# Giving V rows of zero weight an out-of-bound index in a gather-heavy encoder step

## The reference

```
s = jnp.einsum('thcd,hcnd->thcn', q, sub_keys).astype(jnp.float32)
...
top_s, pos = lax.top_k(cand, PEER_TOPK)
expert = jnp.take_along_axis(cidx, pos, axis=-1)
g = jax.nn.softmax(top_s, axis=-1)
u = u_table[expert]
hid = jax.nn.gelu(jnp.einsum('thkd,td->thk', u, xblk).astype(jnp.float32), approximate=False)
v = v_table[expert]
return jnp.einsum('thk,thkd->td', (g * hid).astype(xblk.dtype), v)
```

## Time and profile before

| | |
|---|---|
| median of 3 runs | 3290.63 us (3286.97 to 3292.52) |
| profiled execution, first to last instruction | 3284.0 us |
| POOL busy | 2107.1 us (64%) |
| DVE busy | 1965.5 us (60%) |
| PE busy | 1896.7 us (58%) |
| moved by DMA | 1285.39 MB, 391 GB/s over the span |
| of it by the gathers' queue (q0) | 1143.35 MB in 314032 packets, 88.2% of the DMA engines' time |

### The profile page before, as it was taken

How to read it: one execution, slowest core, us unless ns; L and a number is a source line. 1 busy time by engine, 2 the same in 40 slices (tenths; PEclk the granted TensorE clock), 3 DMA queues, 4 the chain that set the end, 5 groups by cost and what they waited for, 6 DMA issues and landing times. The chain is left out here.

```text
span 3284.0 us, 24041 instructions
## 1 busy us (share of the span) xinstructions
PE 1896.7 (58%) x7901; PEld 735.9 (22%) x7901; DVE 1965.5 (60%) x4492; ACT 348.4 (11%) x787; POOL 2107.1 (64%) x2190
## 2 busy tenths in 40 slices
PE   8976856746843386577543486577644333333546
PEld 4454412333310033332200022322200000000001
DVE  1599695596678844865486744864587645453120
ACT  2221201121100111210100101210100000000000
POOL 0156477566567765775577765775677777777775
PEclk9986978867966588788766698678766665656779
DMA  7699999999999999999999999999999999999998
GB/s 259 228 388 340 404 382 386 402 409 396 405 407 408 386 406 404 409 407 406 398 396 408 396 406 404 410 407 406 388 403 409 387 410 409 409 409 410 409 410 340
DMA packets 384892, 1285.39 MB, mean 391 GB/s; under 512 B 38904, under 2 KB 44672, under 8 KB 384768
## 3 DMA queue, kind: packets, MB, share of 16 engines
q0 software_dynamic: 314032, 1143.35, 88.2%
q1 hardware_dynamic: 68272, 131.60, 11.0%
q10 hardware_dynamic: 2464, 8.91, 0.7%
HBM read 1273.98 MB, written 9.44 MB: 391 GB/s over the span
## 5 line engine op out<-in xcount | busy, mean ns | idle before, releaser
L1069 DVE CUSTOM_DVE_ANT_0 ring<-ring,ps 128x1024 f32<-128x1024 f32 x1088 | 1304.1, 1218 | 990.6 <-DMA ring<-in_peer_u_dram,u_idx 964.7
L1436 PE MATMUL ps<-ring,spread 128*32 128x512 f32 x4352 | 847.1, 892 | 1172.2 <-DMA ring<-in_peer_v_dram,v_idx 1163.1
L706 POOL DMA_INDIRECT ring<-in_peer_u_dram,u_idx x1088 | 1040.0, 956 | 598.3 <-issue 273.7
L706 POOL DMA_INDIRECT ring<-in_peer_v_dram,v_idx x1088 | 1060.5, 975 | 476.6 <-issue 287.0
L1489 PE MATMUL ps<-wbuf,actT 128*128 128x512 f32 (+2 forms) x1536 | 671.8, 592 | 8.0 <-ACT actT L823 3.9
L1436 PEld LDWEIGHTS ps<-ring,spread 128*32 128x32 f32 x4352 | 157.4, 141 | 1779.2 <-DMA ring<-in_peer_v_dram,v_idx 1135.5
L1489 PEld LDWEIGHTS ps<-wbuf,actT 128*128 128x128 f32 (+1 forms) x1536 | 281.8, 189 | 404.8 <-issue 394.3
L1128 DVE MAX8 work<-work 128x8 f32<-128x128 f32 (+3 forms) x432 | 109.2, 322 | 48.5 <-ACT work L994 46.3
L1132 DVE FIND_INDEX8 work<-work 128x8 uint32<-128x128 f32 (+3 forms) x432 | 133.3, 328 | 0.0
L776 ACT COPY spread<-weightT 128x16 f32<-128x16 f32 x64 | 14.2, 224 | 912.7 <-PE ps L1436 872.6
L1069 DVE DVE_READ_ACCUMULATOR2_ANT hidden<- 128x1 f32 x1088 | 89.7, 82 | 0.0
(11 more groups left out here) (189 smaller groups left out, 1179.9 us busy)
## 6 DMA issues: line engine op xcount, KB each, us to landing
wbuf<-in_w_in_dram SPq DMA_DIRECT2D x55, 1024.0 KB, 11.7
wbuf<-in_peer_w_q_dram SPq DMA_DIRECT2D x40, 1024.0 KB, 11.7
wbuf<-in_w_out_dram SPq DMA_DIRECT2D x20, 1024.0 KB, 11.7
ring<-in_peer_u_dram,u_idx POOLq DMA_INDIRECT x1088, 11.6
ring<-in_peer_v_dram,v_idx POOLq DMA_INDIRECT x1088
x_v<-x_scratch ACTq DMA_DIRECT2D x8, 512.0 KB, 6.9
out_dram<-x_v ACTq DMA_DIRECT2D x8, 512.0 KB, 7.3
x_in<-in_x_prompt_dram SPq DMA_DIRECT2D x7, 512.0 KB, 19.6
```

The costliest lines, as they stand in the source:

```text
L706: pool.indirect_dma_start(ring[:, at % RING, :], None, table, bass.IndirectOffsetOnAxis(ap=idx, axis=0)).then_inc(landed, 16)
L1069: ch.put(v_.tensor_tensor_reduce(out=row, in0=row, in1=ux_ps, scale=1.0, scalar=0.0, op0=ALU.mult, op1=ALU.add, accum_out=hidden[:, k:k + ...
L1436: mm = pe.matmul(ps[j:j + 32, B_ACC + c, :], spread[:, at:at + 32], tile[:, 512 * c:512 * c + 512], start=(t % 32 == 0), stop=(t % 32 == 3 ...
```

## The change

A new DVE step `rows_chosen` stands right behind `weights` in DVE's order. It waits for `weightT`, writes 16384 where the transposed weight is exactly zero and 0 elsewhere (one `tensor_scalar`; two for the sample block), adds that to the expert numbers, and signals `v_chosen`. The converted numbers are therefore kept as floats in the same bytes (`v_num`) until this step writes the integers. Each V gather now carries a bound of 16383, and an index over it is not an error, its row is not moved. The first V gather of a block waits for `v_chosen` of that block in the place of `expertT_ready`. `LEAD` goes from 8 to 20, which moves the first V gathers of a block, and the final norm of the block before, back in the list.

```
-LEAD = 8
+LEAD = 20
+EXPERTS = NKEY * NKEY
...
+        v_num = v_idx[:, :, :].bitcast(F32)
...
-            def gather(at, table, idx, landed):
+            def gather(at, table, idx, landed, bound=None):
...
                 pool.indirect_dma_start(ring[:, at % RING, :], None, table,
-                                        bass.IndirectOffsetOnAxis(ap=idx, axis=0)).then_inc(landed, 16)
+                                        bass.IndirectOffsetOnAxis(ap=idx, axis=0), bounds_check=bound,
+                                        oob_is_err=bound is None).then_inc(landed, 16)
...
                     if k == 0:
-                        pool.wait_ge(expertT_ready, b + 1)
-                    gather(order["v", n], v_table, v_idx[:, i, t:t + 1], quad_landed[n // QUAD % QUADS_IN_RING])
+                        pool.wait_ge(v_chosen, b + 1)
+                    gather(order["v", n], v_table, v_idx[:, i, t:t + 1], quad_landed[n // QUAD % QUADS_IN_RING],
+                           EXPERTS - 1)
...
                 elif kind == "weights":
                     weights(b)
+                    rows_chosen(b)
...
+            def rows_chosen(u):
+
+                T, i = rows(u), u % VBUF
+                dve.wait_ge(weightT_ready, u + 1)
+                for half in (slice(0, 64), slice(64, 128)) if u == SAMPLE else (slice(0, P),):
+                    src = weightT[half, u % WTBUF, half] if u == SAMPLE else weightT[:, u % WTBUF, :]
+                    ch.put(v_.tensor_scalar(weight[half, 0:T], src, 0.0, float(EXPERTS), ALU.is_equal, ALU.mult))
+                ch.settle()
+                ch.put(v_.tensor_tensor(v_idx[:, i, 0:T], v_num[:, i, 0:T], weight[:, 0:T], ALU.add), v_chosen)
...
-                ch.put(v_.tensor_copy(v_idx[:, b % VBUF, 0:rows(b)], ps[:, 0, 0:rows(b)]), expertT_ready)
+                ch.put(v_.tensor_copy(v_num[:, b % VBUF, 0:rows(b)], ps[:, 0, 0:rows(b)]), expertT_ready)
```

More of the change, by code:

```diff
@@ L504, in hymba_peer_program @@
         expert_tr, expertT_ready = sem("expert_tr"), sem("expertT_ready")
+        v_chosen = sem("v_chosen")
         dots_done = sem("dots_done")
```

## The result

The changed kernel takes 3213.99 us (median; 3208.72 to 3217.53) against 3289.32 us before: a ratio of 0.977, 95% interval 0.976 to 0.979. It is faster by 75 us, inside the range and on the side that the prediction gave most chance. The gain is less than half of the 167 us that were forecast.

What follows compares the result with a forecast made beforehand. POOL's gather pace of 1.24 us was to bound it once DMA (1.28 us) was relieved: 416 + 2678 (2573 + 97 + 8) + 22 = 3116 us of span, 3122 us median, 5.1% less than 3290.6; range 2950 to 3290 us.

Steps and rivals of the forecast that it cites:

- POOL's own time for 2029 gathers: POOL's floor from 416 us to the last gather: 1.24 us each, 2516 us, plus 57 us for longer gathers.
- waits that come with bytes: In 14 of the 60 us pieces after 416 us DMA ends last, adding 97 us to POOL's floor.
- wait for the weights of block 8: POOL stalls 8 us before block 8's V gathers; the last landing, 11.2 to 3.6 us, was to cancel it.
- The near bounds, +0.10 and -0.14 us: Limits on a bounded V gather's extra POOL time: register write +0.10 us, vanished index handling -0.14 us; zero was taken.
- 0.1 us is worth about 90 us: Each 0.1 us more or less of POOL time per V gather was to move the kernel time by about 90 us.
- rival 2: POOL gets dearer: slower path or register write adds 0.3 us per V gather, 3390 us; chance 13%.
- an estimated 44 us: Extra time over the forecast if each V gather's register write cost POOL 0.05 us and skipped rows saved it nothing.
- in one DVE does, by 8 us: Of the 60 us pieces after 416 us, one has DVE ending last, adding 8 us to POOL's floor.
- Rival 3: Stalls stay: 161 us of POOL waits from PE's and DVE's order replace the 97 us, 3187 us; chance 10%.
- the 34%: Share of V rows taken as left out, between bounds of 26% and 40%; removes 194 MB of 1285 MB.
- The long gathers: Some 60 POOL gathers over 0.94 us, beside DVE's two-input SBUF operations; their 57 us were to stay.
- to about 100: POOL's waits for PE and DVE were to fall from 361 us to about 100, left where weights stream in.

Runs made afterwards that it cites:

- all_skip: The changed kernel with every V row over the bound, so all V rows are left out; 3124.6 us, 0.950 of the kernel before.
- bound_only: The kernel before with only a bound of 16383 on its V gathers, no row left out; 1.009 of the kernel before, on the fourth chip.
- no_skip: The changed kernel with the DVE step adding 0, so no V row is left out; 3327.5 us, 1.012 of the kernel before.
- bound_u: The changed kernel with the bound on U gathers too, no U row left out; 0.998 (third chip) and 1.003 (fourth) of the kernel before.
- one_reg: The changed kernel with the bound written to a register once, not ahead of each V gather; 3209.2 us, 0.976 of the kernel before.
- part_bound: The changed kernel bounded only where weights stream in and on one quad in four elsewhere, block 8 free, one register; 0.990 to 0.991 of before.

## Why the prediction was right in sign and off in size

The forecast span was 3116 us, the trace has 3215.1. Piece by piece:

| piece | forecast | measured | difference |
|---|---|---|---|
| up to gather 147 (counted from 0) | 416 | 417.9 | +2 |
| POOL's own time for 2029 gathers | 2573 | 2636 | +63 |
| waits that come with bytes | 97 | 87 | -10 |
| waits that come with PE's and DVE's order | 8 | 49 | +41 |
| wait for the weights of block 8 | 8 | 11 | +3 |
| behind the last gather | 14 | 15 | +1 |

The measured waits are those of the changed kernel (147 us, of which 11 before block 8), divided by all_skip: what is left there without any V row is put down to order, 49 us, and the rest, 147 - 11 - 49 = 87 us, to bytes. This division holds as far as the two kinds don't cover each other. It may count too much as order, since weights and U rows fill the DMA engines during most of all_skip's waits. The table also charges POOL's 63 us in full; how much of them the waits would have absorbed on this chip, no run shows.

**The term that failed first** is the one named as most likely to: "The near bounds, +0.10 and -0.14 us, lie on both sides of zero, and I take zero". It was +0.05 us, inside the bounds, by 1069 gathers 58 us of the 63 (the rest is in the U gathers). This is the mechanism of rival 2, "The bound may lead the gather through a slower path", at a sixth of the +0.3 us at which it had been priced. What in the handling of a bound takes the time, the traces do not show. Neither of the reasons given for the two bounds held. The register write costs some 4 ns, and indices of rows that stay put cost POOL as much as others. The rule by which "0.1 us is worth about 90 us" stays untested in the changed kernel on the first chip. Every run that bears on it shows less: 29 us for 58 in bound_only, 40 us at most for 63 in no_skip, 9 and 18 us for 53 in bound_u.
The Trainium skill (DMA: Bandwidth & Descriptors, Anatomy of one DMA) gave 50 ns for a dispatch, from which the prediction had an estimated 44 us. That is near the 58 us by chance only, since it was to be the register write's, and one_reg shows that to be nearly free. The other half of that sentence, that skipped rows save POOL nothing, came out: 1028 to 1030 ns at every share of rows left out.

**The second** is "in one DVE does, by 8 us": stretches were cut into 60 us pieces, and each piece given to the engine with the most work in it. That finds an engine that is full for 60 us. It can't see a quad behind 23 us of dense matmuls, as at 887 us above, when PE has time enough over the whole piece. These waits measured 49 us in the place of 8. Rival 3 had this mechanism, with 161 us for it, in 21 waits of over 5 us that end with PE's quads. Of such waits the changed kernel has 7, with 55 us together, and all_skip 2, with 18 us. So most of the 161 us went with the bytes, as the sentence against rival 3 had it, but not all.

**Right.** The bytes (949 MB, with luck in the 34%). The waits that come with bytes, 87 us against 97 us, as far as the division holds; the DMA time behind the 97 us had been taken as falling by a whole row for each row left out, and fell by less (last section). The late start of V in block 0: POOL waited 30.8 us for it and lost 1.7 us by it, gather 147 going at 417.9 us where it went at 416.2 us. LEAD = 20 covered block 1, where LEAD = 8 leaves 11 us. The stall before block 8, its first gather in order of time:

```profile
3115.55 0.26 ACT L751 ACTIVATE hidden<-hidden 128x64 f32<-128x64 f32 x1 [60.89 <-DVE hidden L1085]
3116.15 0.45 DVE L1101 TENSOR_TENSOR weight<-hidden,u_gate 64x64 f32<-64x64 f32 x2
...
3117.17 0.27 ACT L755 COPY weightT<-ps 128x128 f32<-128x128 f32 x1 [1.36 <-PE ps L1433]
3117.47 0.41 DVE L1074 TENSOR_SCALAR weight<-weightT 64x64 f32<-64x64 f32 x2 [0.86 <-ACT weightT L755]
3117.91 0.23 DVE L1076 TENSOR_TENSOR v_idx<-v_idx,weight 128x64 int32<-128x64 f32 x1
3118.94 1.00 POOL L709 DMA_INDIRECT ring<-in_peer_v_dram,v_idx  x1 [11.04 <-DVE v_idx L1076]
```

And the last landing, which had taken 11.24 us, by the chain that ended last:

```profile
3200.50 4.26 DMA ring<-in_peer_v_dram,v_idx
3204.80 3.65 PE ps L1452 x16
```

**The long gathers** beside DVE's operations with two inputs in SBUF: with the DMA engines at 0.64 in the stretch in the place of 0.95 (all_skip) the U and V means are 964 and 1029 ns, as in the changed kernel. Of all_skip's 54 gathers of over 1.2 us, 23 run while the DMA engines are at 0.03 or less, and 40 overlap one of DVE's 40 operations of 128x2048 with two inputs. Full queues are not their cause, and the floor was right to keep them. The rule of the Trainium skill (GPSIMD Engine Reference, Key points) on the shared SBUF interfaces agrees with that; that it is the port and nothing else was not isolated.

**Not right:** POOL's waits in the page's terms did not fall "to about 100" but to 230 us. Part of this is how they were counted: 301 waits contain 0.30 us each that any gather has.

## What to carry to other kernels

Where two limits lie close together, price the change on the second one before counting what it takes off the first: 17% fewer bytes in the gathers' queue were worth 2.3%. Each gather that saved them got 0.05 us longer on the engine that was next, and some of that engine's waits did not go with the bytes. An upper bound for such a change is one kernel that skips everything (3125 us here, more than the 3122 us that had been forecast for a third of the rows). And put the costly form only where its resource ends last, leaving the blocks at the end, whose wait nothing covers, as they were.

## What the runs showed of the hardware

- The bound adds 0.05 us to an indirect DMA of 128 rows of 4 KB (0.94 to 0.99 us where nothing contends), the same at 0, 34, 50 and 100% of rows left out (1028, 1030, 1028 and 1029 ns in the mean).
- A row over the bound still costs the DMA engines a packet: packets under 512 B grow by 47357, 69480 and 139264 at 34, 50 and 100%, the rows left out. q0's time (share by span) is 2905, 2614, 2452 and 1681 us at 0, 34, 50 and 100% of the rows. Per row left out that saves 0.10, 0.10 and 0.14 us of one DMA engine (34, 50, 100%), where a whole row takes 0.167 us (2905 x 16 / 278528). So 0.03 to 0.07 us seem to stay. A part of it may be that packets take longer beside others.
- The page's line "HBM read" shows 1273.98 MB for all of these kernels, also where only 715.59 MB were moved. It does not follow rows that are left out.
- Three of four chips took 7 to 8% longer for the kernel before, and the change is worth 0.2 to 0.4% there instead of 2.3%. A gather that is free to go takes the same 0.94 and 0.99 us. The clock granted to PE is a little lower, 0.73 in the mean of the runs against 0.75, and PE is busy 4% longer (1971 us against 1892 in the changed kernel's traces). What is new is a wait that the trace calls "remote", released by something outside the program's record; no trace of the first chip has one. On the fourth chip, changed kernel:

```profile
POOL ring L709 <- remote: 251.7, 90, 5.0
```

```profile
1798.64 0.99 POOL L709 DMA_INDIRECT ring<-in_peer_v_dram,v_idx  x1 [0.30 <-issue]
1803.81 0.99 POOL L709 DMA_INDIRECT ring<-in_peer_v_dram,v_idx  x1 [4.18 <-remote]
```

  Without the 0.30 us that any gather has, these waits are 225 us. The changed kernel's trace is 315 us longer there than on the first chip, so they are most of the difference and not all: 36 us are lost before gather 147, with 1 us of "remote" among them, and waits for PE grow by 45 us. bound_only, with a DMA share of 0.97, has 88 such waits and the changed kernel, with 0.88, has 90, so they do not go with full DMA engines. That would explain why fewer bytes bring so little there; no run isolates it.
- The "remote" waits are tied to places in the program. In the fourteen traces of these three chips 1030 of them are over 1 us, and 1012 of the 1030 stand ahead of a gather whose number, counted from 0, leaves 3 when divided by 4, for U and V gathers alike. The changed kernel's traces on the fourth and third chip have 75 and 70 of over 1 us, 36 of them at the same gathers. POOL's queue of instruction packets would be a guess, but its packets (71, 80 and 63 for the changed kernel, bound_u and part_bound) do not go with the number of waits (90, 79 and 92), and on the first chip the changed kernel has 71 as well and not one such wait. The cause stays open.
